# Overflow products woven into the gate_up units of their own wide block

## The reference

```python
logits = (x2 @ w_router + b_router).astype(jnp.float32)
top_v, top_i = lax.top_k(logits, TOP_K)              # 4 of 32 experts per token
gates = jax.nn.softmax(top_v, axis=-1)
...
gu = xe @ w_gate_up[e] + b_gate_up[e]                # 1024 -> 2048
gate, up = gu[:, :D_FF], gu[:, D_FF:]
gate = jnp.minimum(gate, SWIGLU_LIMIT)
up = jnp.clip(up, -SWIGLU_LIMIT, SWIGLU_LIMIT)
h = gate * jax.nn.sigmoid(SWIGLU_ALPHA * gate) * (up + 1.0)
return h @ w_down[e] + b_down[e]                     # 1024 -> 1024
```

## Time and profile before

| | us |
|---|---|
| median of three runs | 1349.48 |
| the profiled execution | 1349.23 |
| its span | 1347.4 |
| TensorE busy | 1248.3 (93%) |
| VectorE busy | 831.6 (62%) |
| ScalarE busy | 608.9 (45%) |

### The profile page before, as it was taken

One profiled execution on the slowest core, in us unless ns is written; L12 is line 12 of the kernel. 1 busy time (PEld: TensorE's weight loads), 2 busy tenths in 40 slices (PEclk: granted clock), 3 DMA queues, 4 the chain that ended last, 5 costly groups with the idle time before them and its releaser, 6 DMA issues.

```text
span 1347.4 us, 18886 instructions
## 1 busy us (share of the span) xinstructions
PE 1248.3 (93%) x6184; PEld 807.3 (60%) x6185; DVE 831.6 (62%) x1352; ACT 608.9 (45%) x826; POOL 145.8 (11%) x158
## 2 busy tenths in 40 slices
PE   7999999899999999999999999799999999999992
PEld 5888854477574747464656576264747474656550
DVE  3896668699393837464655596182937464655643
ACT  4111342478273545354444574172735354453632
POOL 8100011010001010101101000100010101101000
PEclk9999999989999999999999999999999999999996
DMA  9610176399999999999999984999999999999984
GB/s 322 87 38 1 52 259 287 131 334 411 355 417 412 419 411 419 405 422 405 414 409 400 416 364 180 406 419 406 421 408 421 404 412 397 401 417 388 421 341 139
DMA packets 67333, 457.16 MB, mean 339 GB/s; under 512 B 15916, under 2 KB 19508, under 8 KB 34520
## 3 DMA queue, kind: packets, MB, share of 16 engines
q1 hardware_dynamic: 56344, 435.28, 78.9%
q0 software_dynamic: 10944, 21.30, 6.7%
HBM read 440.26 MB, written 23.50 MB: 344 GB/s over the span
## 4 chain that ended last, share of the span: by engine, by line
PE 42%; DMA 20%; DVE 8%; issue 5%; ACT 4%; DVEq 0%; SPq 0%; ACTq 0%; POOLq 0%; POOL 0%
PE bank L2144 24%; DMA ring_lo<-in_w_gate_up 15%; PE bank L2254 12%; DVE w_lo L2376 6%; DMA ymix<-ffn_in,idx_next 3%; ACT w_hi L1964 3%; PE bank L2265 2%; DMA token_sums<-ymix,row_cur 1%; PE bank L2134 1%; PE bank L2127 1%; DVE cmix L2394 1%; DVE cmix L2397 1%; PE bank L2230 1%; ACT cmix L1983 0%; PE bank L2274 0%
## 5 line engine op out<-in xcount | busy, mean ns | idle before, releaser
L2376 DVE TENSOR_TENSOR w_lo<-ring_lo,w_hi 128x1024 fp32r<-128x1024 f32 x271 | 315.6, 1220 | 101.0 <-ACT w_hi L1964 99.9
L1964 ACT ACTIVATE w_hi<-ring_lo 128x1024 fp32r<-128x1024 f32 x271 | 270.2, 1052 | 86.8 <-DMA ring_lo<-in_w_gate_up 64.4
L2254 PE MATMUL bank<-ring_lo,x_s 128*64 128x512 f32 x960 | 215.9, 597 | 0.4 <-ACT x_s L1973 0.4
L2144 PE MATMUL bank<-w_hi,x_hi 128*128 128x512 f32 x544 | 179.5, 412 | 8.9 <-DVE x_lo L2382 6.7
L2144 PE MATMUL bank<-w_lo,x_hi 128*128 128x512 f32 x544 | 173.8, 402 | 0.0
L2144 PE MATMUL bank<-w_hi,x_lo 128*128 128x512 f32 x544 | 172.2, 398 | 0.0
L2376 DVE TENSOR_TENSOR w_lo<-w_out,w_hi 128x1024 fp32r<-128x1024 f32 x136 | 161.7, 1220 | 6.0 <-ACT w_hi L1964 5.2
L1964 ACT ACTIVATE w_hi<-w_out 128x1024 fp32r<-128x1024 f32 x136 | 140.0, 1053 | 31.8 <-PE bank L2144 31.6
L1892 POOL DMA_INDIRECT token_sums<-ymix,row_cur x33 | 57.2, 1732 | 742.3 <-ACT ymix L1994 705.3
L2254 PEld LDWEIGHTS bank<-ring_lo,x_s 128*64 128x64 f32 x960 | 65.0, 137 | 119.1 <-issue 117.0
L2144 PEld LDWEIGHTS bank<-w_hi,x_hi 128*128 128x128 f32 x544 | 102.4, 196 | 40.1 <-issue 18.8
(11 more groups left out here) (444 smaller groups left out, 1407.4 us busy)
## 6 DMA issues: line engine op xcount, KB each, us to landing
ring_lo<-in_w_gate_up SPq DMA_DIRECT2D x128, 2048.0 KB, 18.8
w_out<-in_w_down SPq DMA_DIRECT2D x128, 1024.0 KB, 20.5
ring_lo<-in_w_in SPq DMA_DIRECT2D x3, 2048.0 KB, 21.1
w_out<-in_w_out SPq DMA_DIRECT2D x2, 2048.0 KB, 8.7
x<-in_x_prompt SPq DMA_DIRECT2D x6, 512.0 KB, 11.3
bias<-bias_rows SPq DMA_DIRECT2D x132, 3.0 KB
ring_lo<-in_w_in SPq DMA_DIRECT2D x2, 1024.0 KB, 9.7
token_sums<-x SPq DMA_DIRECT2D x4, 512.0 KB
```

The lines of the kernel that those rows point to most:

```text
L1964: nc.scalar.activation(high(j), raw(j), ACT.Copy).then_inc(s["w_hi"], 1)
L2144: last = nc.tensor.matmul(bank[b + u][:], v[:, k, :], part(j)[:, u, :], start=(j == 16 and first), stop=(k == KD - 1 and part is high and ...
L2254: last = nc.tensor.matmul(bank[2 * half][64 * u:64 * u + 64, :], x_s[:, k % 4, 64 * (k // 4):64 * (k // 4) + 64], gu[:, k, :, half, 256 * ...
L2376: v.tensor_tensor(low(j), raw(j), high(j).bitcast(F32), ALU.subtract).then_inc(s["w_lo"], 1)
```

## The change

In block 16, on TensorE, the selection of 17's rows moves from unit 6 to ahead of unit 0; 17's transposes and bias from unit 16 to unit 9; its eight gate_up steps from between units 17 and 18 to ahead of units 11 (two), 12, 13, 14 (two) and 15 (two), into bank 5 instead of 0. The second half of the wide block's own hidden rows goes through bank 7 as before, behind the overflow's, and the selection of 18's rows to unit 20. ScalarE and VectorE follow: VectorE reads off 17's rows at the block's start, and handles the overflow's activation at unit 20, ahead of the second half of the wide block's.

```diff
--- before.py
+++ after.py
@@ -2020,19 +2020,26 @@
         def wide_with_rest(q, side, lq, sq, loads):
 
             for j in range(SLOTS, UNITS):
-                if j == 17:
+                if j == 15:
+                    take_x_quarter(q + 1)
+                elif j == 17:
                     gated(q, lq, 0)
                 elif j == 20:
                     take_h(q, 0)
                 elif j == 21:
-                    gated(q, lq, 1)
+                    act.wait_ge(t["s_used"], t0["s_used"] + LOADS * sq + 4)
+                    act.wait_ge(s["h"], 2 * q + 1)
+                    nc.scalar.activation(g_sb[:, 0:256], bank[5][:, 0:256], ACT.Gelu_apprx_sigmoid).then_inc(s["sig"], 2)
+                    act.wait_ge(s["w_used"], UNITS * lq + 16)
+                    act.wait_ge(s["h"], 2 * q + 3)
+                    nc.scalar.activation(g_sb, bank[2][:], ACT.Gelu_apprx_sigmoid).then_inc(s["sig"], 1)
                 elif j == 22:
-                    take_x_quarter(q + 1)
+                    act.wait_ge(s["hT_psum"], 2 * q + 3)
+                    nc.scalar.activation(h_s[:, 0:2, :].rearrange("p j t -> p (j t)"), bank[1][:, 0:256], ACT.Copy).then_inc(s["h_hi"], 2)
                 elif j == 23:
-                    take_h(q, 1)
+                    act.wait_ge(s["hT_psum"], 2 * q + 4)
+                    nc.scalar.activation(h_hi[:, 4:8, :].rearrange("p k t -> p (k t)"), bank[7][:], ACT.Copy).then_inc(s["h_hi"], 1)
                 split(loads, lq, j)
-            act.wait_ge(s["h"], 2 * q + 2)
-            quarter_hidden(q + 1, sq, bank[1])
             act.wait_ge(s["w_used"], UNITS * lq + UNITS)
             take_y(q, side, [4, 5], [512, 512])
             take_x_small(q + 2)
...
@@ -2195,27 +2199,32 @@
         def wide_with_rest(q, lq, sq, e_rest, e_next):
 
             pe.wait_ge(s["x_lo"], lq + 1)
+            select(e_rest, q + 1)
             for j in range(UNITS):
-                if j == 6:
-                    select(e_rest, q + 1)
+                if j == 9:
+                    pe.wait_ge(s["idx"], q + 2)
+                    pe.wait_ge(s["y_free"], q + 1)
+                    x_transposes(q + 1, 4)
+                    set_bias_quarter(q + 1, bank[5], bank[4])
+                if j == 11:
+                    pe.wait_ge(t["x_s"], t0["x_s"] + sq + 1)
+                for k in {11: (0, 1), 12: (2,), 13: (3,), 14: (4, 5), 15: (6, 7)}.get(j, ()):
+                    quarter_gate_up(k, bank[5])
                 if j == 14:
                     h_transposes(q, 0)
                 if j == 16:
                     pe.wait_ge(s["h_lo"], 2 * lq + 1)
-                    pe.wait_ge(s["y_free"], q + 1)
-                    pe.wait_ge(s["idx"], q + 2)
-                    x_transposes(q + 1, 4)
-                    set_bias_quarter(q + 1)
+                    pe.wait_ge(s["h"], 2 * q + 3)
+                    quarter_h_transposes(bank[1])
                 if j == 18:
-                    h_transposes(q, 1)
-                    pe.wait_ge(t["x_s"], t0["x_s"] + sq + 1)
-                    for k in range(KD):
-                        quarter_gate_up(k)
-                        if k == 5:
-                            pe.wait_ge(s["h_lo"], 2 * lq + 2)
-                            select(e_next, q + 2)
+                    pe.wait_ge(s["h"], 2 * q + 4)
+                    for k in range(4):
+                        c = 2 * P * (k // 2) + k % 2
+                        last = nc.tensor.transpose(bank[7][:, k * P:(k + 1) * P], h_sb[:, c:c + 2 * P - 1:2], ident[:])
+                    last.then_inc(s["hT_psum"], 1)
                 if j == 20:
-                    quarter_h_transposes(q + 1, bank[1])
+                    pe.wait_ge(s["h_lo"], 2 * lq + 2)
+                    select(e_next, q + 2)
                 products(lq, j)
             pe.wait_ge(s["h_hi"], 2 * q + 4)
             for k in range(KD):
@@ -2224,16 +2233,15 @@
             x_transposes(q + 2, 2)
             set_bias_small(q + 2)
 
-        def quarter_gate_up(k):
+        def quarter_gate_up(k, sums):
 
             for c in range(4):
-                last = nc.tensor.matmul(bank[0][32 * c:32 * c + 32, :], x_s[:, k % 2, 32 * (k // 2):32 * (k // 2) + 32],
+                last = nc.tensor.matmul(sums[32 * c:32 * c + 32, :], x_s[:, k % 2, 32 * (k // 2):32 * (k // 2) + 32],
                                         gu[:, k, :, c // 2, 256 * (c % 2):256 * (c % 2) + 256], start=False, stop=(k == KD - 1))
             if k % 2 == 1:
                 last.then_inc(t["s_used"], 1)
 
-
...
@@ -2454,35 +2463,42 @@
             for j in range(2, SLOTS):
                 split(lq, j)
 
-        def quarter_swiglu(q):
-            dve.wait_ge(s["sig"], 2 * q + 2)
-            v.tensor_scalar(u_sb[:, 0:256], bank[0][:, 256:512], LIMIT + 1.0, 1.0 - LIMIT, ALU.min, ALU.max).then_inc(s["clip"], 2)
-            dve.wait_ge(s["clip"], 2 * q + 2)
+        def quarter_swiglu(sums, count):
+            dve.wait_ge(s["sig"], count)
+            v.tensor_scalar(u_sb[:, 0:256], sums[:, 256:512], LIMIT + 1.0, 1.0 - LIMIT, ALU.min, ALU.max).then_inc(s["clip"], 2)
+            dve.wait_ge(s["clip"], count)
             v.scalar_tensor_tensor(out=h_sb[:, 0:256], in0=g_sb[:, 0:256], scalar=GATE_MAX, in1=u_sb[:, 0:256], op0=ALU.min, op1=ALU.mult).then_inc(s["h"], 2)
 
         def wide_with_rest(q, side, lq, sq, e_rest, e_next):
 
             pick(e_rest, tb["full"][:, 0:1], 4)
+            next_slots(q, side, 4, sq)
             for j in range(SLOTS, UNITS):
-                if j == 11:
-                    next_slots(q, side, 4, sq)
-                elif j == 17:
+                if j == 17:
                     swiglu(q, lq, 0)
                 elif j == 20:
                     take_h(q, 0)
+                    quarter_swiglu(bank[5], 2 * q + 3)
                 elif j == 21:
-                    swiglu(q, lq, 1)
+                    dve.wait_ge(s["w_used"], UNITS * lq + 16)
+                    dve.wait_ge(s["h"], 2 * q + 3)
+                    v.tensor_scalar(u_sb, bank[3][:], LIMIT + 1.0, 1.0 - LIMIT, ALU.min, ALU.max).then_inc(s["clip"], 1)
+                    dve.wait_ge(s["clip"], 2 * q + 4)
+                    dve.wait_ge(s["sig"], 2 * q + 4)
+                    dve.wait_ge(s["hT_psum"], 2 * q + 3)
+                    v.scalar_tensor_tensor(out=h_sb, in0=g_sb, scalar=GATE_MAX, in1=u_sb, op0=ALU.min, op1=ALU.mult).then_inc(s["h"], 1)
+                    pick(e_next, zero[:, 0:1], 2)
                 elif j == 23:
-                    take_h(q, 1)
+                    dve.wait_ge(s["h_hi"], 2 * q + 4)
+                    v.tensor_tensor(h_lo[:, 4:8, :].rearrange("p k t -> p (k t)"), bank[7][:],
+                                    h_hi[:, 4:8, :].rearrange("p k t -> p (k t)").bitcast(F32), ALU.subtract).then_inc(s["h_lo"], 1)
                 split(lq, j)
-            pick(e_next, zero[:, 0:1], 2)
             next_slots(q + 1, 1 - side, 2, sq + 1)
-            quarter_swiglu(q + 1)
 
         def quarter(q, sq, e_next, base):
 
             pick(e_next, base, 4)
-            quarter_swiglu(q)
+            quarter_swiglu(bank[0], 2 * q + 2)
             next_slots(q, 0, 4, sq + 1, blocks_back=1)
 
         def over(b):
```

More of the change, by code:

```diff
@@ L2064, in small, with quarter @@
                 split(loads + 1, lq, 5)
-        def quarter_hidden(q, sq, turned):
+        def quarter(q, sq):
             act.wait_ge(t["s_used"], t0["s_used"] + LOADS * sq + 4)
@@ L2153, in set_bias, with set_bias_quarter @@
             last.then_inc(s["bias_used"], 1)
-        def set_bias_quarter(q):
+        def set_bias_quarter(q, sums, idle):
             pe.wait_ge(t["bias_in"], 64 * q + (t0["bias_in"] + 64))
-            nc.tensor.transpose(bank[1][:, 0:P], ident[:], ident[:])
+            nc.tensor.transpose(idle[:, 0:P], ident[:], ident[:])
             for c in range(4):
-                last = nc.tensor.matmul(bank[0][32 * c:32 * c + 32, :], tb["one_b"][32 * c:32 * c + 3, 0:1].to_broadcast([3, 32]),
+                last = nc.tensor.matmul(sums[32 * c:32 * c + 32, :], tb["one_b"][32 * c:32 * c + 3, 0:1].to_broadcast([3, 32]),
                                         tb["bias"][32 * c:32 * c + 3, :], start=True, stop=False)
@@ L2282, in quarter @@
                     pe.wait_ge(landed[k // 2], 16 * loads)
-                quarter_gate_up(k)
+                quarter_gate_up(k, bank[0])
                 if k == 1:
@@ L2286, in quarter @@
             pe.wait_ge(s["y_free"], q + 1)
-            quarter_h_transposes(q, bank[5])
+            pe.wait_ge(s["h"], 2 * q + 2)
+            quarter_h_transposes(bank[5])
             pe.wait_ge(s["h_hi"], 2 * q + 2)
@@ L2325, in over @@
         def over(b):
-            set_bias_quarter(b + NPOS)
+            set_bias_quarter(b + NPOS, bank[0], bank[1])
             quarter(b + NPOS, b + (EARLY + LATE + 2), b + NPOS, over_expert(pe, b + 1))
```

7 lines of the change are left out of this document (2 added, 5 removed).

## The result

The changed kernel takes **1355.68 us** (median of 5 runs, 1352.62 to 1357.86) against 1349.48 (1349.21 to 1349.87): a ratio of 1.0050, 95% interval 1.0040 to 1.0061. It is 6.2 us slower where no change was forecast, and above the range of 1345.0 to 1353.0. The profiled execution has a span of 1353.9 us.

What follows compares the result with a forecast made beforehand. The prediction took transfers and TensorE's chain to bound the kernel together, meeting at 920 us. Between - 1.1 and + 0.3 it took - 0.5: 1348.7, plus 0.25 for the median, 1349.0 us; range 1345.0 to 1353.0.

Steps and rivals of the forecast that it cites:

- (a): Block 16's start: TensorE waits at the moved selection for VectorE's one-hot matrix; + 4.15 us.
- (b): Behind the stop at block 16's start: TensorE's clock falls; + 1.6 us, bounds 0 and 5.1.
- (c): Woven gate_up steps in block 16: five more returns to big products, + 0.6 us; old transposes' stop goes, - 0.52.
- (d): New waits in block 16 ahead of units 16 and 20, + 0.3 us each; overflow's gather at unit 9, 0.
- D: The time by which block 16 ends later; forecast 6.4 us, bounds 4.2 and 13.
- (e): Transfers of block 18's loads: head start used up by the hole before the down loads; + 0.3 us.
- D - 6.1: General form of the transfers' delay at block 18's down loads; + 0.3 us for the forecast D.
- (f): TensorE, blocks 18 to 19: stop for 19's rows shrinks from 8.43 to 1.7 us; block 19's start - 1.1.
- (g): Both chains at block 20: between - 1.1 and + 0.3 us, taken as - 0.5, passed on to the end.
- Rival 3: Slower: clock low behind block 16's opening stop loses 5.1 us instead of 1.6, transfers late; 1353.3 us; chance 0.22.
- Rival 1: Faster: the stop before block 19 goes altogether, block 20 starts at 914.4; 1345.8 us; chance 0.16.
- Rival 2: Faster: block 16's selection does not wait, transfers gain 4 to 5 us; 1344.8 us; chance 0.08.

Runs made afterwards that it cites:

- e5: On e1, the overflow's transposes and bias moved to ahead of unit 12, its gate_up steps to ahead of units 13, 14 and 15; 1348.62 us.
- e7: The kernel before with only the gather of 19 issued ahead of the scatter of 17 on GpSimd; 1349.60 us.
- e6: e5 with the gather of 19 issued ahead of the scatter of 17 on GpSimd; 1345.56 us.
- e3: The changed kernel with 34 unused transposes ahead of the selection, to keep TensorE busy in the stop; 1352.15 us.
- e1: The changed kernel with the selection of 17's rows ahead of unit 3 instead of unit 0; 1354.58 us.
- e9b: The changed kernel with the gather of 19 issued ahead of the scatter of 17 on GpSimd; 1351.69 us.
- e10b: e2 with the gather of 19 issued ahead of the scatter of 17 on GpSimd; 1356.23 us.
- e4: On e1, the overflow's down products woven in too, two steps ahead of each of units 20, 21 and 22; 1354.79 us.
- e2: The kernel before with only the selection hoisted ahead of unit 0 and VectorE's reading off behind its pick, no weaving; 1356.09 us.

## Why the prediction was wrong

**What bounds the kernel: right.** That at 920 us both chains meet, and that a gain on one alone is worth next to nothing, is what e5 (transfers early, no gain) and e7 (TensorE early, no gain) show, and e6 shows the gain of both.

**(a) The stop: right**, 4.05 us for 3.9. By block 14's start the first unit comes 4.7 us later for 4.15; the selecting products themselves ran at the low clock (0.55 from start to start for 0.28).

**(b) The clock: mis-sized.** Six pairs and part of a seventh at half speed cost 5.27 - 2.73 + 0.27 = 2.8 us for the 1.6 taken, within the bounds of 0 and 5.1. e3 measures the same 2.8. I had taken the value of the nearer of two rows, though this stop was nearly twice as long as that one's; midway between the bounds would have been 2.6.

**(c), (d) Weaving: mis-sized a little.** A unit between two woven steps takes 1.60 us (823.23 to 824.83) instead of 1.36. Its first pair takes 0.58, the return that I had priced, but its last takes 0.56 too (824.27 to 824.83), the way over to the overflow's products, which I had put at nothing. Together 0.24 for 0.12; five are 1.2 for 0.6. The waits ahead of units 16 and 20 came to 0.42 and nothing, for 0.3 and 0.3. The gathered rows of the overflow were there at unit 9, but only since the block was late, which is luck; e1 shows the wait.

Together D was 8.8 or 8.9 where 6.4 was forecast, with the bounds of 4.2 and 13 around it.

**(e) The transfers: mis-sized by 1.5 us.** The rule D - 6.1 comes out as D - 4.6 (e6), where it can be seen. For D = 8.8 that is +4.2 for the forecast's own +2.7. A part is the restart at the down loads: in the changed kernel the DMA share is 0.29 from 851 to 853 us and 0.89 from 853 to 855, so about 1.2 us behind the issue at 851.41 are empty, for the 0.7 taken. The rest is open. The other figure that the prediction names here, a fixed cost of about 2 us from the Trainium skill, "DMA: Bandwidth & Descriptors", section on the anatomy of one DMA, would have given D - 4.8, near what was measured. But that section gives it for transfers that GpSimd issues, while these are the sync engine's, and no row tells where such a cost falls, so that it comes near is no evidence for it. This chain does not set the end here.

**(f) TensorE's chain: this step failed.** I let the scatter of 16 take 9 us and the gather of 19 take 11, because the load queue in front of them would be shorter. They took 11.41 and 15.07, so the stop stayed at 8.11 instead of 1.7, and block 20 came 7.8 us later by block 14's start, instead of 1.1 earlier. Of these 8.9 us, 6.4 are the stop (8.11 less 1.7: 2.4 from the scatter and 4.1 from the gather) and 2.4 are D.

The swap runs show what the gather's time hangs on: put ahead of the scatter of 17 on GpSimd, it lands in 10.7 us in e6 (857.42 to 868.13) and in e9b (861.69 to 872.38), with full transfers beside it, and in 10.6 and 10.9 in e7 and e10b. Behind that scatter it takes 14.8 to 15.3 us in all eight kernels. The 15 us are 10.7 and some 4.3 behind the scatter, and how far the load queue reaches shows in neither.

The Trainium skill, "DMA: Bandwidth & Descriptors", section on queues, rings and completion order, lets each DMA engine take packets in turn from every queue that has work; by that rule the prediction gave the gather 15 us, and set it aside because gathers range from 2.8 to 16.5 us. The trace agrees with the rule, 15.07, and the range does not speak against it: the rule is about whether the other queue has work at all, not how much, and a part of the range is what stands ahead in the gather's own queue (the gather of 21, behind the fuller scatter of 19, takes 16.5 us before: 922.56 to 939.04). I read a spread over all 33 gathers as a law of the queue's length, when the row for this very gather gave 14.95.

The scatter is told apart less well. In e4 it was issued at 855.08, behind the issue of all four down loads, and the copy behind it ran at 862.88: 7.8 us instead of 11.4. The next load was issued only at 859.45, and from 855 to 857 us the DMA share was 0.86, while in the changed kernel the four down loads were issued around the scatter (from 851.41 us on) and the share in the same window was full. So 9 us and less do occur, and the short load queue that I had counted on may be what brings them about; with one case it is not shown.

**(g) Together: failed with (f).** I took - 0.5, between the two chains, though the later one sets the end. The sum should have been made as the larger of the two chains, with each given its own D. With D = 8.8 and the gather as before, TensorE's chain would have been read off at once: +8.8 less what later stops give back.
What they give back was missing from the sum too. In the kernel before TensorE stands once more for rows, ahead of block 21:

```profile
922.56 1.06 POOL L1884 DMA_INDIRECT ymix<-ffn_in,idx_next  x1 [0.30 <-issue]
...
939.08 1.10 PE L2127 MATMUL bank<-ident,ymix 128*128 128x128 f32 x8 [2.06 <-DMA ymix<-ffn_in,idx_next]
```

In the changed kernel the same transposes, at 944.91 above, have no idle time: the gather of 21, issued at 930.51, meets the third hole and lands in time, within 14.4 us instead of 16.5. The shift falls from 7.8 at block 20 to 5.7 at 22 and is 6.5 at 32. e2 and e6, without that hole, have the stop still: 2.07 and 2.05 us.

**The rivals.** Rival 3 had the sign, and its condition, D from 8.8 on, was just met; but it named the clock alone (5.1 us) and the transfers, and both were wrong: the clock cost 2.8, and the transfers had slack. Its price, 1353.3, is 2.4 below the time. Rival 1 is what e6 brought about, by another edit. Rival 2 did not happen; e5 comes near its premise (D of 1.2) and shows that its gain of 4 to 5 us is not paid out without TensorE's chain. A rival was missing: that both chains carry D because nothing in the stop for 19's rows shrinks.

## What to carry to other kernels

Where two chains meet, work out each one's shift to the meeting point by itself, from rows of that very wait, and take the later; a saving on one is paid out only when the other has slack, and a hole in the transfers further on is the sign of it. Before an operation is hoisted, look at when its input is ready on the other engine: the stop of 4 us in a full TensorE cost itself and 2.8 us of low clock. And a gather that TensorE waits for should be issued ahead of scatters that nobody waits for, though this gave time only where the transfers had slack (e6 and e9b, not e7 and e10b).
